# Norms by token tile in separate PSUM banks, rotary tables made earlier, and identity products on TensorE between stages

## What is computed

```python
for l in range(2):                       # first block
    y = hybrid_mixer(x, ...)
    x = layer_norm(DN_ALPHA * x + y, ln1_g[l], ln1_b[l])
    y = conv_gated_ffn(x, ...)
    x = layer_norm(DN_ALPHA * x + y, ln2_g[l], ln2_b[l])
for l in range(2):                       # second block
    h = rmsnorm(x, norm_mix[l])
    ...                                  # three branches, gated, merged; rope from positions
    x = x + merged @ w_out[l]
    h = rmsnorm(x, norm_ffn[l])
    x = x + (silu(gate(h)) * up(h)) @ w_ffn_out[l]
out = rmsnorm(x, norm_final)
```

## Time and profile before

| | |
|---|---|
| median of 3 runs | 2322.86 us (2319.32 to 2325.93) |
| time of the profiled execution | 2316.84 us |
| its span in the profile | 2315.0 us |
| PE busy, weight loads busy | 94%, 87% |
| POOL, ACT, DVE busy | 65%, 46%, 41% |

### The profile page before, as it was taken

The page is one execution under the profiler, slowest core; times in us unless marked ns, Lnnn a source line. Parts: engine busy times, 40 slices in busy tenths (PEclk is TensorE's granted clock), DMA queues, the critical chain, the costliest instruction groups (busy, mean ns, idle before and its releaser), DMA issues.

```text
span 2315.0 us, 35984 instructions
## 1 busy us (share of the span) xinstructions
PE 2173.9 (94%) x15336; PEld 2008.9 (87%) x15336; DVE 945.6 (41%) x1484; ACT 1076.2 (46%) x1519; POOL 1499.2 (65%) x632
## 2 busy tenths in 40 slices
PE   8999989999878989989999999999999899999998
PEld 7789978799778979879999899888789789998998
DVE  5352356432476536365112211456364561123112
ACT  4555555555555252245444444472532354544444
POOL 6689877698844233356778788663333567687886
PEclk9999989999988989999999999999999999999999
DMA  8336544355523122234445455432122344354553
GB/s 338 139 129 217 184 136 152 122 185 188 183 92 120 55 73 74 86 127 140 158 161 185 149 186 190 150 128 82 65 92 74 109 146 164 130 185 159 182 184 135
DMA packets 47183, 333.05 MB, mean 144 GB/s; under 512 B 5168, under 2 KB 5552, under 8 KB 7856
## 3 DMA queue, kind: packets, MB, share of 16 engines
q1 hardware_dynamic: 47024, 330.76, 41.4%
HBM read 329.69 MB, written 1.05 MB: 143 GB/s over the span
## 4 chain that ended last, share of the span: by engine, by line
PE 60%; DVE 8%; ACT 3%; issue 2%; POOL 0%; DVEq 0%; ACTq 0%
PE bank L147 14%; PE bank L149 13%; PE bank L148 13%; PE y L147 2%; PE y L149 2%; PE y L148 2%; PE bank L1738 2%; PE bank L1748 1%; DVE conv L1384 1%; PE bank L1747 1%; PE bank L1671 1%; DVE sc L2347 1%; PE bank L1790 1%; PE bank L1793 1%; PE bank L1566 1%
## 5 line engine op out<-in xcount | busy, mean ns | idle before, releaser
L348 POOL TENSOR_TENSOR w_lo<-w_raw,w_hi 128x1024 fp32r<-128x1024 f32 x602 | 1463.6, 2437 | 798.3 <-ACT w_hi L339 798.2
L339 ACT ACTIVATE w_hi<-w_raw 128x1024 fp32r<-128x1024 f32 x602 | 636.4, 1059 | 1038.6 <-PE bank L149 868.2
L147 PE MATMUL bank<-x_hi,w_hi 128*128 128x256 f32 x2960 | 878.7, 297 | 27.8 <-POOL w_lo L348 17.1
L148 PE MATMUL bank<-x_lo,w_hi 128*128 128x256 f32 x2960 | 849.3, 287 | 0.0
L149 PE MATMUL bank<-x_hi,w_lo 128*128 128x256 f32 x2960 | 849.0, 287 | 0.0
L147 PEld LDWEIGHTS bank<-x_hi,w_hi 128*128 128x128 f32 x2960 | 580.0, 196 | 53.2 <-issue 25.5
L148 PEld LDWEIGHTS bank<-x_lo,w_hi 128*128 128x128 f32 x2960 | 580.4, 196 | 10.5 <-issue 8.6
L149 PEld LDWEIGHTS bank<-x_hi,w_lo 128*128 128x128 f32 x2960 | 579.2, 196 | 0.0
L876 DVE SCALAR_TENSOR_TENSOR conv<-bank,par_sb,conv 128x254 f32<-128x254 f32 (+1 forms) x176 | 76.8, 478 | 239.8 <-ACT conv L864 238.3
L1246 DVE TENSOR_TENSOR hid_lo<-hid,hid_hi 128x512 fp32r<-128x512 f32 x22 | 45.1, 2049 | 241.2 <-ACT hid_hi L1241 241.2
L147 PE MATMUL y<-w_hi,hid_hi 128*128 128x512 f32 x352 | 139.9, 397 | 3.3 <-DVE hid_lo L898 3.3
(11 more groups left out here) (397 smaller groups left out, 3250.8 us busy)
## 6 DMA issues: line engine op xcount, KB each, us to landing
...
```

What stands on the lines that cost most here:

```text
L147: pe.matmul(out, lhs[0], rhs[0], start=start, stop=False, skip_group_check=skip)
L148: pe.matmul(out, lhs[0], rhs[1], start=False, stop=False, skip_group_check=skip)
L339: act.activation(self.hi[:, h % HALVES, :], self.raw[:, n % RAWS, i * HW:(i + 1) * HW], ACT.Copy).then_inc(*sig.up("high", h))
L348: pool.tensor_tensor(self.lo[:, h % HALVES, :], self.raw[:, n % RAWS, i * HW:(i + 1) * HW], self.hi[:, h % HALVES, :].bitcast(F32), ALU.su ...
```

## The change

1. **Norms by tile.** Turned tile `tt` goes to banks 4*tt to 4*tt+3 (`turn_tile`); ACT and DVE evict pieces of 128x128 per chunk, tile 0 first on ACT, in the order `TILES` on DVE. The normalised rows of tile 0 are made by ACT (all of them in `Norm1`, half in `Norm2`). `Norm2` takes the sum of squares on ACT instead of `bn_stats` on DVE. The root's table is loaded ahead.
2. **Last products by tile.** `by_tokens` now covers the last two halves ahead of each norm and the last four ahead of the joint of the blocks, where three `down` products are also moved behind the last `conv` units.
3. **The joint of the blocks** is one stage, `Border`, that works tile by tile. Each affine step is folded into two instructions instead of three.
4. **Identity products.** `repeat` issues products of the identity with itself into a free bank: 8 ahead of tile 0 and 4 ahead of tile 1 in `Norm1`, 7 ahead of tile 1 in `Norm2`, 16 and 7 in `Border`; and 12 products of 128x256 at the program's start.
5. **ACT's weight halves.** Ahead of a norm ACT issues one weight half fewer; the fourth half of the next stage (`high` of last+4) follows the evictions.
6. **Rotary tables** are made in `Feed1` of layer 1; `positions` is loaded there.

```diff
+    def by_tokens(self, last, count):
+
+        first = last + 1 - count
+        group = range(first, last + 1)
+        self.parts[2 * first:2 * (last + 1)] = [(h, part) for part in range(2) for h in group]
...
@@ Norm1
+        net.repeat(pe, net.bank[3], 8)
+        turn_tile(net, pe, k_l, self.tb, net.xn, 0)
+        pe.wait_ge(*sig.at("var", *k_l, 1))
+        net.repeat(pe, net.bank[4], 4)
+        turn_tile(net, pe, k_l, self.tb, net.xn, 1)
...
+        main.act(act, self.end() - 4)
+        act.preload_act_table_set("sqrt_and_others")
+        main.act(act, self.end() - 2)
+        root(0)
+        act.wait_ge(*sig.at("inverse", *k_l))
+        act.wait_ge(*sig.at("product", self.after().last))
+        for half in range(2):
+            c = slice(half * HALF, (half + 1) * HALF)
+            act.activation(net.xn[:, 0, c], net.xtok[:, 0, c], ACT.Identity, scale=net.rs[:, 0:1], bias=net.sd[:, 0:1]
+                           ).then_inc(*sig.up("xn_act", *k_l, 0, half))
+        root(1)
+        for tt in range(TT):
+            for i in range(4):
+                features(tt, i)
+        main.act(act, self.end())
...
+TILES = [(0, 0), (0, 1), (1, 0), (0, 2), (1, 1), (0, 3), (1, 2), (1, 3)]
+
+
+def turn_tile(net, pe, k_l, tb, xn, tt):
+    for k in range(KD):
+        if k % 4 == 0:
+            by_act = tt == 0 and (k or k_l not in DVE_FIRST)
+            pe.wait_ge(*net.sig.at("xn_act" if by_act else "xn", *k_l, tt, k // 4))
+        mm = pe.transpose(tb[tt][k // 2][:, (k % 2) * P:(k % 2 + 1) * P], xn[:, tt, k * P:(k + 1) * P],
+                          net.K("ident"))
...
@@ Norm2
+        turn_tile(net, pe, k_l, self.tb, net.xn2, 0)
+        pe.wait_ge(*sig.at("x_new", *k_l, 1, 1))
+        net.repeat(pe, net.bank[4], 7)
+        turn_tile(net, pe, k_l, self.tb, net.xn2, 1)
...
+                act.activation(net.xn2[:, tt, c], net.xtok[:, tt, c], ACT.Square, accum_out=net.bn[:, tt, half, 0:1]
...
+        main.act(act, self.end() - 4)
+        act.preload_act_table_set("sqrt_and_others")
+        root(0)
+        act.wait_ge(*sig.at("inverse", *k_l))
+        act.activation(net.xn2[:, 0, HALF:D], net.xtok[:, 0, HALF:D], ACT.Copy, scale=net.rs[:, 0:1]
+                       ).then_inc(*sig.up("xn_act", *k_l, 0, 1))
+        main.act(act, self.end() - 2)
+        root(1)
         for tt in range(TT):
...
@@ Border
+        net.repeat(pe, net.bank[3], 16)
+        turn_tile(net, pe, self.second, self.tb, net.xn, 0)
+        pe.wait_ge(*sig.at("var", *self.first, 1))
+        net.repeat(pe, net.bank[4], 7)
+        turn_tile(net, pe, self.second, self.tb, net.xn, 1)
...
+        statistics(0, 0)
+        statistics(0, 1)
+        variance(0)
+        normed(0)
+        statistics(1, 0)
+        square(0)
+        statistics(1, 1)
+        variance(1)
+        inverse(0).then_inc(*sig.up("inverse", *self.second))
+        normed(1)
+        square(1)
+        step(inverse(1))
...
@@ Mixer2
-        if l == 0:
-            act.wait_ge(*sig.at("reduced"))
-            act.activation(net.tables[:, 2:4, :], m["angle"][:, :, :], ACT.Sin).then_inc(*sig.up("sined", 0))
-            act.activation(m["half_sine"][:, :, :], m["angle"][:, :, :], ACT.Sin, scale=0.5).then_inc(*sig.up("sined", 1))
...
@@ Net
+    def repeat(self, pe, bank, times):
+
+        for _ in range(times):
+            pe.matmul(bank[:, 0:P], self.K("ident"), self.K("ident"), start=True, stop=True)
...
+                pe.wait_ge(*sig.at("ones_set", "x"))
+                for _ in range(12):
+                    pe.matmul(self.bank[7][:, 0:T], self.x[:, 0, 0:P], self.x[:, 0, :], start=True, stop=True)
```

More of the change, by code:

```diff
@@ L1034, in before @@
+        for tt, i in TILES:
+            low(tt, i)
     def before(self):
@@ L1054, in sp @@
         net, sig = self.net, self.net.sig
-        net.main.send(sp, net.main.halves[self.after().last][0] + 1 + (5 if self.last else 12 if self.key == "ln1" else 9))
+        net.main.send(sp, net.main.halves[self.after().last][0] + 1 + (12 if self.key == "ln1" else 9))
         if self.l == 0:
@@ L1117, in dve, with residual @@
         step = net.dve_chain.step
-        if self.after is not None:
-            net.main.dve(dve, self.end())
-        for tt in range(TT):
+        def residual(tt, half):
+            c = slice(half * HALF, (half + 1) * HALF)
+            if tt == TT - 1 and half == 1:
+                dve.wait_ge(*sig.at("product", self.after().last))
+            else:
+                dve.wait_ge(*sig.at("summed", self.more, tt, half))
+            dve.tensor_tensor(net.xtok[:, tt, c], net.xtok[:, tt, c], net.y[:, tt * D + half * HALF:tt * D + (half + 1) * HALF],
+                              ALU.add).then_inc(*sig.up("x_new", *k_l, tt, half))
@@ new lines, in act @@
+        act.preload_act_table_set("sqrt_and_others")
+        root_first(0)
+        main.act(act, self.end() - 2)
+        squares(0)
+        root(0)
+        root_first(1)
+        act.wait_ge(*sig.at("inverse", *self.second))
+        for half in range(2):
+            c = slice(half * HALF, (half + 1) * HALF)
+            act.activation(net.xn[:, 0, c], net.xtok[:, 0, c], ACT.Copy, scale=net.rs[:, 0:1]
+                           ).then_inc(*sig.up("xn_act", *self.second, 0, half))
+        act.wait_ge(*sig.at("par2_loaded"))
@@ L1150, in pool @@
+        for tt, i in TILES:
+            low_part(net, dve, self.second, self.tb, self.gain, tt, i)
     def pool(self, pool):
-        if self.after is not None:
-            self.net.main.pool(pool, self.end())
+        self.net.main.pool(pool, self.end())
     def sp(self, sp):
-        return
+        self.net.main.send(sp, self.net.main.halves[self.after().last][0] + 1 + 5)
 class Final:
@@ L2427, in __init__ @@
         self.main = Stream(sig, raw, hi, lo, units)
-        self.main.by_tokens(len(self.main.halves) - HALVES)
+        for s in self.stages:
+            if isinstance(s, (Border, Final)):
+                self.main.by_tokens(s.after().last, HALVES)
+            elif isinstance(s, (Norm1, Norm2)):
+                self.main.by_tokens(s.after().last, 2)
     def K(self, name):
@@ L2595, in _ @@
                 for s in self.stages:
-                    if isinstance(s, (Norm1, Norm2, Mixer2, Final)):
+                    if isinstance(s, (Norm1, Feed1, Border, Norm2, Mixer2, Final)):
                         s.sp(sp)
```

409 lines of the change are left out of this document (248 added, 161 removed).

## The result

The changed kernel is slower. Its median is 2327.62 us (2323.34 to 2333.28, 20 runs) against 2318.46 (2316.36 to 2325.93, 20 runs) for the kernel before: ratio 1.0036, 95% interval 1.0028 to 1.0044. I had forecast 2298, a gain of 25 us on the 2322.86 that the kernel before then had over three runs, and gave slower 0.02.

What follows compares the result with a forecast made beforehand. PE, busy 94% of the span, was taken as the bound. Gains 6.0+8.4+9.4+5.2 = 29.0, less 4 for the clock, gave 25.0: 2316.84 to 2291.8, and 2298 with the median 6.0 above the profile; range 2288 to 2307.

Steps and rivals of the forecast that it cites:

- slower 0.02: Rival: `positions` lands late in `Feed1` 1 and delays DVE and PE, making the kernel slower; chance 0.02.
- the clock term of 4 us: PE restarts at the joints: 4 us deducted for slow clock, between 0 and 10.8 for seven slow restarts.
- What POOL allows: `Feed1` 0 behind `ln1`: POOL's slack lets the stages take up 0.86+1.2 = 2.06 us, so the 2.0 gain just fits.
- `Norm1` term (6.0): Three norms of `Norm1`: first weight half ends at T+12.1 against 14.1, gaining 2.0 us each, 6.0 in all.
- I count 0: Rotary tables in `Feed1` 1: ACT's two passes and DVE's dozen small ones lie under PE's weight products, costing 0.
- The 5.2 for `Mixer2` 0: Start of `Mixer2` 0: removing the rotary tables gains 3.8+1.4 = 5.2 us.
- The joint (9.4): Joint of the blocks: first weight half ends at T+14.0 against 23.4, a gain of 9.4 us.
- Its new rows at T-0.05: Joint of the blocks: six passes and the folded affine form give tile 0's new rows at T-0.05.
- `Norm2` (8.4): Three norms of `Norm2`: first weight half ends at T+10.1, gaining 2.3 twice and 3.8 once, 8.4 us.
- The row decides: PE clock at joints: trace rows, where turns help keep the clock (4 us), preferred over the skill's page (10.8 us).
- the width of evictions: `Norm1` evictions of 128 columns: 0.37 us each taken, between 0.37 and 0.47.
- the repeats' price: Identity products on PE: 0.11 us each, costing nothing unless each took over 0.27 us.

Runs made afterwards that it cites:

- all, not filled: Changed kernel with ACT's early weight half and POOL's wait in `Norm1`, POOL held back at the joint, angle passes behind units 9, 12, 15; 2306.65 us.
- the three last combinations: Changed kernel with early high part, quiet joint, later angle passes; `Norm2` repeats 14 and 6, as in the change, or no repeats anywhere: 2303.39, 2306.65, 2310.41 us.
- the last combination: Changed kernel with early high part, quiet joint, angle passes behind units 9, 12, 15, and no identity products or twelve products at the start; 2310.41 us.
- quiet `Norm1`: Changed kernel, but POOL waits in `Norm1` for DVE's last low piece before the low part of last+4 and `x_tok`; 2327.22 us, ratio 1.003.
- late tables: Changed kernel with angle passes behind units 9, 12 and 15 of `Feed1` 1, sines behind 17, cosines behind 21; 2327.09 us, ratio 1.0029.

## Why the prediction was wrong

What failed is the cover: I took DVE's passes at the price that they have while POOL is idle, in `Norm1`, at the joint and for the rotary tables (counted as 0), and in the changed program they stand beside POOL's weight halves, where each can take 2 us more. Second comes the clock term of 4 us, which was too small.

**"What POOL allows" and the `Norm1` term (6.0): wrong in sign.** I let POOL's `low` of last+4 stand behind ACT's evictions and counted it as a gift: POOL quiet for tile 1's rows. I didn't ask what else DVE does when it starts, at T+10.7. It takes DVE's last piece, 3.82 us for 0.72. With POOL's half moved under the statistics the joint ends at T+12.9 against 12.1 foreseen, so the 3.1 us from there to T+16.0 are this one collision, and about 1.1 us more are the second stretch at 1.2 GHz behind it. It isn't the whole miss: without the collision the three norms gained 2.0 us, not 6.0. About half of the missing 4.0 is the restart at half clock, which my sum had at full clock (where such a half ran at 1.00, in "all, not filled", it ended at T+12.6). The rest is the 0.5 us from there to my 12.1, three times, and a before that was shorter at the two twins than the 14.1 I took for them. The earlier trace rows had such a collision: the same pass in 1.00 and 2.71 us. I read it as a property of two rows, not of every pass of that kind. The Trainium skill (SBUF — State Buffer, SBUF: two separate sides) says that DVE and GpSimd share a pair of ports, which one instruction holds to its end while the other fully blocks, if DVE runs a two-port mode or has two SBUF inputs. The trace agrees: 2.45 for 0.29 on a cast, and 0.69 beside POOL where an input was in PSUM. POOL pays as well, 13.67/5 = 2.73 for 2.40.

**Work beyond the joint: not in the sum.** `Mixer1` 1 lost 4.4 by the backlog of POOL that I had weighed only as weight halves late for PE. It came through DVE instead: the pass that PE waited for took 2.72 us for 0.69 beside POOL's half at 380.02.

**"I count 0" for the tables in `Feed1` 1: 7.1.** "A dozen small ones" were small with POOL idle, 4.5 us; beside it they were 17.2. The 5.2 for `Mixer2` 0 was right: 5.3.

**The joint (9.4): 3.5.** "Its new rows at T-0.05" costed the folded form at POOL's quiet. With POOL held back the joint was worth 9.0, so the chain was right and the cover wrong. In the three last combinations it was worth 6.7 to 7.5, because the first half behind it ran at 0.50 to 0.62.

**`Norm2` (8.4): 0.3 in all.** Weights came 0.8 us later than foreseen (a one-column addition of DVE took 1.19 beside POOL), and the first half took 5.25 for 3.08. Here the clock term is what failed: I had 4 for seven joints, and filling these three alone shortened them by 1.74 each, 5.2. "The row decides" was wrong as a rule: turns had been followed by clock 1.00 in the kernel before, and weren't here, with seven repeats or, in the last combination, with none. In `Norm2` repeats kept it where they left no hole. Behind the joint of the blocks the half took 3.51 with them and 4.47 without in the changed kernel, but 4.47 and 5.29 with the same repeats in two of the combinations, so there they are no warrant. The Trainium skill's rule that I set against it (TensorE: Matmul & The Clock Gate, Part 4: PE-mode transpose) fits the restarts in `Norm2`, though not the two restarts of before.

**Right**: the width of evictions, the time of the restart in `Norm1`, the repeats' price (0.23 us each at full clock, twice my 0.11, still under cover), nothing from the start.

**What stays open.** The mended stages shift the median less than their profiles say (quiet `Norm1` 9 us, late tables 7, both within 1 us of the changed kernel), while the combinations keep their gain. The unprofiled runs of one kernel spread by up to 29 us, and with them the mean clock; which of `Mixer2`'s waits meets the lower clock differs from profile to profile with the same instructions. I haven't found what sets it. So the split of the 9 us by stage is that of one execution. The 11.2 gained in `Mixer2` 0 came in no other profile, and I had foreseen nothing there; that it hides part of the loss is luck of this execution or a property of this kernel, which its one profile can't tell. The 7.6 lost in `Mixer2` 1, where I had foreseen nothing, came back in eight of thirteen profiles, so it may belong to the change, but no run shows how, and there is only one profile of before to set against it. The losses in `Norm1` and `Mixer1` 1 were undone in the trace by one edit and that in `Feed1` 1 by another, so these are shown.
